# Sixteen expert weight slots in a loop over pairs, 8192-byte runs, evened late pieces, and a new seam and end

## The reference

```python
def trunk_layer(x, mod, ...):
    sh1, sc1, g1, sh2, sc2, g2 = jnp.split(mod[:, None, :].astype(x.dtype), N_MOD, axis=-1)
    h = rmsnorm(x, norm1_g) * (1 + sc1) + sh1
    p = jnp.einsum('bnd,de->bne', h, w_in)
    ...                                   # differential and grouped-query attention
    x = x + g1 * jnp.einsum('bne,ed->bnd', o, w_out)
    h2 = rmsnorm(x, norm2_g) * (1 + sc2) + sh2
    x = x + g2 * ec_moe(h2, w_router, w_gate, w_up, w_down)
    return x, own_kv

def ec_moe(h, w_router, w_gate, w_up, w_down):   # 16 experts, width 1024
    aff = jax.nn.softmax(jnp.einsum('bnd,de->bne', h, w_router), axis=-1)
    gate, idx = lax.top_k(jnp.swapaxes(aff, 1, 2), cap)       # 64 latent + 16 context rows each
    xs = jax.vmap(lambda hb, ib: hb[ib])(h, idx)
    hid = jax.nn.silu(jnp.einsum('becd,edf->becf', xs, w_gate)) * jnp.einsum('becd,edf->becf', xs, w_up)
    out = jnp.einsum('becf,efd->becd', hid, w_down) * gate[..., None]
    ...                                   # added back to the rows idx
```

## Time and profile before

| | |
|---|---|
| median of 3 runs | 2313.69 us (2310.33 to 2314.91) |
| the profiled execution | 2312.74 us, span 2310.9 |
| mean granted TensorE clock | 0.966 |
| busy share of the span | PE 92%, PEld 50%, DVE 36%, ACT 24%, POOL 7% |
| the chain that ended last | PE 76%, DMA 15%, DVE 5%, issue 2%, ACT 1% |
| DMA | 623.69 MB, mean 270 GB/s over the span |
| output projection | first product at 887.69, last residual done at 1171.2 |
| experts | first product at 1213.87, last at 2266.75 |
| instruction packets (q8) | 50, 0.82 MB |

### The profile page before, as it was taken

The page is one execution under the profiler, slowest core; times in us unless marked ns, Lnnn a source line. Parts: engine busy times, 40 slices in busy tenths (PEclk is TensorE's granted clock), DMA queues, the critical chain, the costliest instruction groups (busy, mean ns, idle before and its releaser), DMA issues.

```text
span 2310.9 us, 35984 instructions
## 1 busy us (share of the span) xinstructions
PE 2136.7 (92%) x15265; PEld 1166.9 (50%) x15265; DVE 836.6 (36%) x1292; ACT 551.0 (24%) x977; POOL 173.3 (7%) x236
## 2 busy tenths in 40 slices
PE   5899999999999988899939999999999999999992
PEld 2568887778777766678833333333222233222230
DVE  3259888135566666675351101101101011010112
ACT  4432222222266663111110111111101111110112
POOL 1020100000000001121010000000000000000001
PEclk8999999999999997899969999999999999999996
DMA  9966665642300007555478999999999999999995
GB/s 371 324 221 211 216 229 217 236 147 73 130 1 1 1 1 252 165 172 161 171 198 334 392 391 393 399 399 393 405 395 395 392 392 401 397 403 394 394 404 227
DMA packets 160109, 623.69 MB, mean 270 GB/s; under 512 B 13016, under 2 KB 14536, under 8 KB 131968
## 3 DMA queue, kind: packets, MB, share of 16 engines
q1 hardware_dynamic: 135344, 498.65, 55.8%
q0 software_dynamic: 20688, 107.74, 14.8%
q10 hardware_dynamic: 4000, 16.26, 2.0%
HBM read 593.07 MB, written 29.54 MB: 269 GB/s over the span
## 4 chain that ended last, share of the span: by engine, by line
PE 76%; DMA 15%; DVE 5%; issue 2%; ACT 1%; SPq 1%; POOL 0%; ACTq 0%; POOLq 0%; DVEq 0%
PE ps L1019 24%; PE ps L1026 12%; PE ps L589 9%; PE ps L591 9%; PE ps L590 9%; DMA arena<-in_w_expert_up 8%; DMA arena<-in_w_mod 3%; PE ps L839 3%; PE ps L873 3%; PE ps L774 1%; PE ps L856 1%; DMA r_d<-rstd 1%; DMA arena<-mod_d 1%; PE ps L860 1%; DVE arena L1800 1%
## 5 line engine op out<-in xcount | busy, mean ns | idle before, releaser
L1019 PE MATMUL ps<-arena 128*32 128x512 f32 x6144 | 707.6, 594 | 16.0 <-DMA arena<-in_w_expert_up 9.9
L1019 PEld LDWEIGHTS ps<-arena 128*32 128x32 f32 x6144 | 193.3, 110 | 468.2 <-issue 409.7
L1026 PE MATMUL ps<-arena 128*32 128x512 f32 x3072 | 371.0, 593 | 0.0
L589 PE MATMUL ps<-B_w_hi,B_x_hi 128*128 128x512 f32 x720 | 288.0, 400 | 2.7 <-ACT arena L1142 1.5
L591 PE MATMUL ps<-B_w_lo,B_x_hi 128*128 128x512 f32 x720 | 282.1, 392 | 0.0
L590 PE MATMUL ps<-B_w_hi,B_x_lo 128*128 128x512 f32 x720 | 281.8, 391 | 0.0
L1026 PEld LDWEIGHTS ps<-arena 128*32 128x32 f32 x3072 | 98.1, 110 | 223.0 <-issue 223.0
L1906 DVE SCALAR_TENSOR_TENSOR arena<-arena,gcol 80x2048 f32<-80x2048 f32 x16 | 37.6, 2348 | 352.5 <-ACT arena L1339 352.5
L589 PEld LDWEIGHTS ps<-B_w_hi,B_x_hi 128*128 128x128 f32 x720 | 136.1, 189 | 45.4 <-issue 11.6
L1679 DVE TENSOR_TENSOR B_w_lo<-arena,B_w_hi 128x1024 fp32r<-128x1024 f32 x72 | 87.5, 1221 | 186.3 <-ACT B_w_hi L1182 186.1
L591 PEld LDWEIGHTS ps<-B_w_lo,B_x_hi 128*128 128x128 f32 x720 | 135.9, 189 | 29.4
(11 more groups left out here) (214 smaller groups left out, 2014.7 us busy)
## 6 DMA issues: line engine op xcount, KB each, us to landing
arena<-in_w_expert_gate SPq DMA_DIRECT2D x128, 1024.0 KB, 21.1
arena<-in_w_expert_up SPq DMA_DIRECT2D x128, 1024.0 KB, 19.2
arena<-in_w_expert_down SPq DMA_DIRECT2D x128, 1024.0 KB, 21.2
arena<-in_w_mod POOLq DMA_DIRECT2D x48, 1024.0 KB, 5.7
arena<-in_w_in SPq DMA_DIRECT2D x36, 1024.0 KB, 5.2
arena<-in_w_mod SPq DMA_DIRECT2D x64, 512.0 KB, 9.5
arena<-in_w_out SPq DMA_DIRECT2D x16, 1024.0 KB, 6.1
arena<-in_w_mod POOLq DMA_DIRECT2D x64, 256.0 KB, 3.1
```

The source lines that it names most:

```text
L589: eng.matmul(out, x_hi, w_hi, start=start, stop=False)
L1019: mm = pe.matmul(bank(b)[32 * q:32 * q + 32, :], rows[:, 32 * (q % 2):32 * (q % 2) + 32], w_pair[q // 2], start=start, stop=stop, skip_gro ...
L1026: mm = pe.matmul(bank(b)[32 * q:32 * q + 32, :], rows, w_four[q], start=start, stop=stop, skip_group_check=True)
```

## The change

- `RING_E` goes from 12 to 16; the four new slots lie where `x1` lies, so chunks 11 to 15 of expert 0 wait until `x1` is stored. 24 chunks are no multiple of 16 but 48 are, so the loops of SP and TensorE take two experts per turn.
- A gate or up chunk holds, per partition, two neighbouring rows of the matrix: one run of 8192 bytes in place of two of 4096. The contraction index is then paired (row 2p + r of each 256), and everything that meets it is too: router weights, norm2 gain, shift and scale of the second norm (a new step `paired` with two small loads and two transposes at the start), raw transposes and the gathered rows are read with a step of two elements.
- `x1_d` rows get 16 words more, which hold `rstd2`; `r_d` and its gather go. The scaled rows are written to `xsP`, apart from the gathered `xs`. `final_g` is loaded after the first gathered rows are scaled.
- `LATE_AT` and `LATE_SUM_AT` are new, late pieces come after `take_raw`, and the transposition of g2 moves from half 24 to half 30.
- In w_down context goes ahead of latent for f = 3 to 7. ACT copies two of the four context parts, DVE the other two, both ahead of the latent copies; DVE scales in two halves.
- At the end SP issues the loads of `acc_d`, and DVE makes the mean of the next tile ahead of the scaling of this one.

```diff
-RING_E = 12
+RING_E = 16
+EARLY_E = 11
+ROW_PAD = 16
-LATE_AT = {1: 4, 2: 4, 3: 4, 4: 4, 5: 4, 6: 4, 9: 4, 10: 4, 11: 4, 12: 3, 13: 3, 14: 3, 17: 4, 18: 3, 19: 3, 20: 3, 21: 3, 22: 3}
-LATE_SUM_AT = {5: 0, 11: 1, 18: 2, 23: 3}
+LATE_AT = {1: 3, 2: 3, 3: 3, 4: 3, 5: 3, 6: 1, 7: 2, 8: 2, 9: 3, 10: 3, 11: 3, 12: 3,
+           13: 3, 14: 3, 15: 2, 16: 2, 17: 3, 18: 3, 19: 3, 20: 3, 21: 3, 22: 3, 23: 2, 24: 2}
+LATE_SUM_AT = {7: 0, 13: 1, 19: 2, 25: 3}
...
-        x1_d = nc.dram_tensor("x1_d", [TOK, D], F32, kind="Internal").ap()
-        r_d = nc.dram_tensor("r_d", [TOK, 1], F32, kind="Internal").ap()
+        x1_d = nc.dram_tensor("x1_d", [TOK, D + ROW_PAD], F32, kind="Internal").ap()
...
-                L0 + 3 * SLOT, L0 + 4 * SLOT, K0, Q0 + 4 * SLOT]
+                L0 + 3 * SLOT, L0 + 4 * SLOT, K0, Q0 + 4 * SLOT, Q0, Q0 + SLOT, Q0 + 2 * SLOT, Q0 + 3 * SLOT]
...
-        wg_v = w_gate.rearrange("o e (q i p) n -> (o e) q p i n", i=2, p=P)
-        wu_v = w_up.rearrange("o e (q i p) n -> (o e) q p i n", i=2, p=P)
+        wg_v = w_gate.rearrange("o e (q p r) n -> (o e) q p (r n)", r=2, p=P)
+        wu_v = w_up.rearrange("o e (q p r) n -> (o e) q p (r n)", r=2, p=P)
...
+        def by_pairs(v):
+            return v.rearrange("q (i p r) -> q i r p", p=P, r=2)
...
-            chunk_e(0, RING_E - 1)
-            for j in range(RING_E, XCH):
-                sp.wait_ge(xused, j - RING_E + 1)
-                chunk_e(0, j)
-            with sp.Fori(1, NE) as e:
-                for j in range(XCH):
-                    sp.wait_ge(xused, e * XCH + (j - RING_E + 1))
-                    chunk_e(e, j)
+            for j in range(EARLY_E, RING_E):
+                chunk_e(0, 0, j)
+            for c in range(RING_E, 2 * XCH):
+                sp.wait_ge(xused, c - RING_E + 1)
+                chunk_e(c // XCH, c // XCH, c % XCH)
+            with sp.Fori(1, NE // 2) as e2:
+                for c in range(2 * XCH):
+                    sp.wait_ge(xused, e2 * (2 * XCH) + (c - RING_E + 1))
+                    chunk_e(e2 * 2 + c // XCH, c // XCH, c % XCH)
+            sp.wait_ge(scattered, 16 * NE)
+            for t in range(NT):
+                sp.dma_start(x1[:, t, :], acc_d[P * t:P * (t + 1), :]).then_inc(x_in[t], 16)
...
+                rows = by_pairs(x1[:, t, NB * n:NB * (n + 1)])
                 for c in range(4):
-                    k = 4 * n + c
-                    mm = pe.transpose(bank(5 + i % 2)[:, P * c:P * (c + 1)], x1[:, t, P * k:P * (k + 1)], ident[:, :])
+                    mm = pe.transpose(bank(5 + i % 2)[:, P * c:P * (c + 1)], rows[:, c // 2, c % 2, :], ident[:, :])
...
-            with pe.Fori(0, NE) as e:
-                for i in range(6):
...
+            with pe.Fori(0, NE // 2) as e2:
+                for h in range(2):
+                    e = e2 * 2 + h
+                    for i in range(6):
...
+                    for f in range(3, 8):
+                        landed(e2, h, 16 + f)
+                        mm = context_down(h, f)
+                        if f == 7:
+                            mm.then_inc(con_out, 1)
+                        latent_down(h, f, 0)
+                        latent_down(h, f, 1).then_inc(xused, 1)
...
-                act.dma_start(r_d[P * t:P * (t + 1), :], rstd2[:, t:t + 1]).then_inc(r_stored, 16)
+                act.dma_start(x1_d[P * t:P * (t + 1), D:], rstdP[:, t, :]).then_inc(r_stored, 16)
...
+                act.activation(xsP[0:CAP, cols].rearrange("c (i r p) -> c i r p", r=2, p=P), by_pairs(xs[0:CAP, cols]), ACT.Copy,
+                               scale=xs[0:CAP, D:D + 1]).then_inc(xs_scaled, 1)
...
-                act.wait_ge(lat_out, e + 1)
-                for h in range(2):
-                    act.activation(xrow_out[0:CL, 2 * NB * h:2 * NB * (h + 1)], bank(4, 2)[CL * h:CL * (h + 1), :], ACT.Copy)
+                act.wait_ge(con_out, e + 1)
+                for n in range(2):
+                    act.activation(xrow_out[CL:CAP, NB * n:NB * (n + 1)], bank(6)[CXP * n:CXP * n + CX, :], ACT.Copy)
                 act.wait_ge(xused, e * XCH + 24)
-                for n in range(4):
-                    ins = act.activation(xrow_out[CL:CAP, NB * n:NB * (n + 1)], bank(6)[CXP * n:CXP * n + CX, :], ACT.Copy)
-                ins.then_inc(y_taken, 1)
+                act.activation(xrow_out[0:CL, 0:2 * NB], bank(4, 2)[0:CL, :], ACT.Copy).then_inc(half_taken, 1)
+                act.activation(xrow_out[0:CL, 2 * NB:4 * NB], bank(4, 2)[CL:2 * CL, :], ACT.Copy).then_inc(y_taken, 1)
...
-                pool.indirect_dma_start(rC[:, :], None, r_d[:, :],
-                                        bass.IndirectOffsetOnAxis(ap=idxC[:, e:e + 1], axis=0)).then_inc(r_gathered, 16)
...
+                    dve.wait_ge(logits_done, 3 * NT - 1)
...
+                for _ in range(LATE_AT.get(i, 0)):
+                    late_piece(late)
+                    late += 1
...
+                dve.wait_ge(row_free, e + 1)
+                dve.wait_ge(con_out, e + 1)
+                for n in range(2, 4):
+                    ins = dve.tensor_copy(xrow_out[CL:CAP, NB * n:NB * (n + 1)], bank(6)[CXP * n:CXP * n + CX, :])
+                ins.then_inc(con_taken, 1)
...
+                for h, taken, at_least in ((0, half_taken, e + 1), (1, y_taken, e + 2)):
+                    cs = slice(2 * NB * h, 2 * NB * (h + 1))
+                    dve.wait_ge(taken, at_least)
+                    ins = dve.scalar_tensor_tensor(out=xrow_out[0:CAP, cs], in0=xrow_out[0:CAP, cs], scalar=gcol[:, 0:1],
+                                                   in1=G2[0:CAP, cs], op0=ALU.mult, op1=ALU.mult)
...
+            final_mean(0)
+            for t in range(NT):
+                if t + 1 < NT:
+                    final_mean(t + 1)
                 dve.wait_ge(frstd_ready, t + 1)
```

244 lines of the change are left out of this document (126 added, 118 removed).

## The result

The changed kernel took 2337.02 us (median of 4 runs, 2334.68 to 2340.15), the kernel before on the same chip 2312.01 (4 runs, 2308.54 to 2314.91): a ratio of 1.011 with a 95% interval of 1.0089 to 1.013. It is 1.1% slower, which is clear of the noise, outside the predicted range, and 68 us from the predicted time. The profiled execution has a span of 2338.3 us against 2310.9, 27.4 more.

A forecast was written before the change was run, and what follows sets the result against it. It took the first six experts as bound by TensorE and the last nine by the weight stream. 2312.7 - 20 - 3 - 21 + 5 - 6 = 2267.7, forecast as 2269 us for the median of runs; range 2255 to 2293.

The forecast's parts named there:

- Looped in pairs: Expert loop: TensorE's doubled body must be fetched at seven jumps, 0.7 us seen each, 5 us more (0 to 48).
- The fetch eats everything: Rival at the expert loop's jumps: 6.8 us idle plus 2.4 of half clock each, 64 us, 2328; chance 0.05.
- A dearer fetch: Rival at the expert loop's jumps: about 6 us per fetch, 4.1 shown, 29 in all, 2293; chance 0.12.
- Late pieces: Output projection: at most three late pieces per half cut TensorE's idle time and half clock, 20 us less (10 to 25).
- Seam: Between top-k and first expert: one gather replaces two and is issued earlier, 3 us less.
- Ring and runs: Expert stage: sixteen slots and 8192-byte runs together remove all load stalls of the stream-bound experts, 21 us less.
- End: After the last matmul: fewer copies, halved scaling, earlier means and loads issued by SP, 6 us less (4 to 6.5).

The follow-up runs named there:

- the unrolled kernels: Two variants of the changed kernel with TensorE's experts written out: sixteen slots, 2276.91 us; twelve slots, 2286.04 us.
- no loop: The changed kernel with TensorE's expert pairs written out one behind the other, ring of sixteen kept: 2276.91 us, ratio 0.983.
- the ring of twelve with the single body: The changed kernel with twelve slots and TensorE and SyncE looping over single experts, all else kept: 2273.10 us, ratio 0.9811.
- the kernel with seven blocks: The changed kernel with 24 transposes ahead of the loop, three of four context products and half the latent down products left out: 2267.00 us (one run).

## Why the prediction was wrong

**Looped in pairs** is the step that failed. "2.6 us: 0.7 seen, 7 x 0.7 = 5 us" was written for what costs 10.6 a jump, 74 in all. Three things in it were wrong. The price was taken near the 2.5 us of a 4 KB store because "A fetch is one packet, not eighty rows"; the branch takes 6.1 us under the full stream and 3.7 under half of it, and 3.5 to 3.7 of the 6.1 pass before the packet starts to move. One packet is not one wait: the body began so near a block's end that a second block was needed 15 matmuls later, a gap of 1.8 to 3.2 us. And half clock after the gaps costs 4.1 us a jump, more than either gap; the step counted it at 2.4 in the other-side rival and at nothing in the forecast. Both ends of the bound, 0 and 48, missed the measured 74.

The rival on the other side, "The fetch eats everything", named the mechanism and the place and gave 2328; the result is 2337. Its deciding point, 4.7 us idle per jump, is passed: 3.85 and 1.84 are 5.7 at the first jump, and the mean is 6.4. The result is so close by luck: its single gap of 6.8 us stands for two, and its 2.4 us of half clock for 4.1; the sums, 9.2 and 10.6, are nearer than the parts. Its chance of 0.05 leaned on "Against it: a single 16 KB packet", and that is the sentence that should have gone. The rows had the doubt in them: an instruction queue silent for 960 us and a body doubled past what was known to stay. "A dearer fetch" at 2293 had the branch's 6 us right and one gap and the clock missing.

The Trainium skill, "Runtime: NRT & Kernel Launch", section "Instruction fetch mechanics", gives TensorE 128 KiB, 2048 instructions, in blocks of 256, and says that a taken branch to a target outside the current window of two pages must fetch before execution goes on. By the block size and the fetch the trace agrees, and 2,424 instructions are over the figure. The two pages do not fit TensorE: the single body of 1,213 instructions, more than four blocks, jumps back with no packet on q8 in 960 us. But bodies of 2,040 and 1,848 instructions are under the 2048 and are fetched too, the latter even where they touch eight blocks only; 1,592 in seven blocks stay. The measurement decides: what stays is less than the figure, and a body is safe only up to seven blocks, the largest that was seen to stay. The same section warns that branches are costly and gives no price; here it is 4.8 to 10.6 us per jump under the full stream. Its sentence that crossing into a next block is mostly hidden holds for TensorE in the unrolled kernels, which never wait for an instruction, and not for the stream beside it.

**Late pieces** (-20) was right: -20.6 in the changed kernel and -19.9 alone, from the output projection's first product to the cast. **Seam** (-3): from the cast to the first matmul 10.8 us instead of 14.8, -4.0. The gather was issued 1.1 us behind the cast and landed in 5.8 us, under the 7 that was taken.

**Ring and runs** (-21) was right in the changed kernel for another reason than the forecast's: its experts without a jump read 64.3 to 64.6 to the last, because the jumps give the stream 74 us to catch up. Without jumps it depends on the fetches. With sixteen slots and no fetches (seven blocks) 1.8 us of load waits stay, so the term is -20 and its reason holds; with sixteen slots and 71 more packets (no loop) 14 us stay, and with twelve slots and no fetches 10. The stream needs 65.9 us per expert and not 65.6. What the forecast lacked here is that fetched instructions slow the stream even where TensorE waits for none.

**End** (-6) came out at -4.65. The scaling's 3.7 us and the tiles' 2.54 us period are nearly as predicted (3.5 and 2.5). What was missed is that taking the mean of the next tile ahead of the first scaling makes the first scaling wait for the second square: it starts 4.6 us behind the first square's start instead of 3.0 (2318.70 - 2314.12 against 2289.64 - 2286.67). Of the 2.1 us that the shorter periods bring, 1.6 go there. From the scaling's end to the first square it is 11.7 us instead of 12.9, so loads issued by SP go with 1.3 less, where 0 to 0.5 was charged.

Without the one step the sum would have been 2338.3 - 74 = 2264 for the span; the ring of twelve with the single body has 2268.2, and the kernel with seven blocks 2265.2.

## What to carry to other kernels

Before a loop body grows, look at the instruction queue: if it is silent while the loop runs, the body stays on the engine, and that is worth keeping; here seven blocks of 256 instructions stayed, eight did not, and each jump then cost 4.8 to 10.6 us under a full weight stream. If a ring needs a longer period than the loop body can hold, take the ring that fits the single body: twelve slots and one expert per turn kept all but some 8 us of what the kernel with seven blocks and sixteen slots reaches (load waits of 9.7 us against 1.8). And where one wait goes and another comes in the same stage, ask which hides the other: in the changed kernel the jumps let the stream catch up, so its experts without load waits said nothing on the ring. Last, before a few microseconds are put down to an edit, look where the stage started: here it moved by up to 9 us between executions with the same code ahead of it.

## What the runs showed of the hardware

A taken branch for which TensorE had to fetch took 6.1 us under a full weight stream and 3.7 us (median) under half of one. The 16 KB packet itself moved for 1.1 us and started 3.5 to 3.7 us behind the branch's start, under half the stream mostly 1.0. The 32 matmuls behind the first jump ran at half clock (7.4 us instead of 3.4). Where the target lay shortly ahead of a block's end, a second gap of 1.8 to 3.2 us followed behind 15 matmuls; moving the loop by 48 instructions took 4.6 us off each jump.

TensorE kept a body of 1,592 instructions (seven blocks of 256) and did not keep one of 1,848 (eight). With 71 more packets of 16 KB fetched, stream-bound experts took up to 1.6 us longer, though TensorE never waited for an instruction.

Loads in rows of 8192 bytes need 65.9 us for an expert's 24 chunks where gate and up in rows of 4096 need 66.7. Four products of 32 rows into one bank take as long as one of them. GpSimd's power of one column takes 0.58 us alone and ends only 0.4 us after VectorE's running scaling where they overlap.
